# The recurrence of a decoder layer: the y gate kept in two places, its product on VectorE, and the first projection of the merge in two pieces

## What is computed

```python
xc = conv_b + sum(xpad[:, k:k + s] * conv_w[k] for k in range(4))      # causal, per channel
r  = sigmoid(einsum(xc by blocks of 128, w_rg) + b_rg)
ig = sigmoid(einsum(xc by blocks of 128, w_ig) + b_ig)
a  = exp(-8 * r * softplus(-lambda))
gated_x = sqrt(1 - a*a) * (ig * xc)
h  = linear scan over positions:  h[t] = a[t] * h[t-1] + gated_x[t]
o_lru = (h * gelu(yb)) @ w_o_lru
merged = sigmoid(gate_mla) * o_mla + sigmoid(gate_lru) * o_lru
```

## Time and profile before

| | |
|---|---|
| median of 3 runs | 2469.99 us (2469.56 to 2472.95) |
| the profiled execution | span 2469.3 us; the page gives no other time for it |
| PE busy | 2341.7 us, 95% |
| DVE / ACT / POOL busy | 40% / 35% / 14% |
| recurrence, from the first to the last sigmoid of a group | 814.16 to 1003.29 us |

### The profile page before, as it was taken

The page is one execution under the profiler, slowest core; times in us unless marked ns, Lnnn a source line. Parts: engine busy times, 40 slices in busy tenths (PEclk is TensorE's granted clock), DMA queues, the critical chain, the costliest instruction groups (busy, mean ns, idle before and its releaser), DMA issues.

```text
span 2469.3 us, 25993 instructions
## 1 busy us (share of the span) xinstructions
PE 2341.7 (95%) x10629; PEld 1940.8 (79%) x10629; DVE 983.4 (40%) x1089; ACT 859.0 (35%) x1233; POOL 339.0 (14%) x372
## 2 busy tenths in 40 slices
PE   7999999999997999899999788989999999999997
PEld 6888888888786877688887677767888888888885
DVE  3334433432335554211213788465342233322333
ACT  3322223322223666411323566344332223222222
POOL 0000000200003232200012455332210000200002
PEclk9999999999999999999999899999999999999998
DMA  5333433443232111122410100445433423343221
GB/s 179 93 104 100 139 94 94 128 128 102 87 98 77 47 39 48 52 77 68 122 40 20 27 14 21 171 162 167 123 103 102 137 94 94 121 130 107 94 100 62
DMA packets 278016, 232.55 MB, mean 94 GB/s; under 512 B 22853, under 2 KB 250250, under 8 KB 277898
## 3 DMA queue, kind: packets, MB, share of 16 engines
q1 hardware_dynamic: 277898, 230.89, 30.3%
HBM read 209.36 MB, written 20.97 MB: 93 GB/s over the span
## 4 chain that ended last, share of the span: by engine, by line
PE 80%; issue 7%; POOL 5%; DVE 4%; ACT 3%; DMA 1%; SPq 0%; POOLq 0%; ACTq 0%; DVEq 0%
PE ps L85 26%; PE ps L86 26%; PE ps L87 26%; POOL r_xc L841 1%; PE ps L320 1%; POOL r_xc L835 1%; POOL r_xc L838 1%; PE ps L1459 1%; PE ps L1491 1%; ACT a_probs L1435 1%; POOL a_rot L1376 1%; POOL b_sum L1631 1%; ACT w_hi L91 0%; POOL x L287 0%; DVE a_s L1425 0%
## 5 line engine op out<-in xcount | busy, mean ns | idle before, releaser
L85 PE MATMUL ps<-u_hi,w_hi 128*128 128x512 f32 x1920 | 753.0, 392 | 15.5 <-ACT r_gate_y L761 9.5
L87 PE MATMUL ps<-u_hi,w_lo 128*128 128x512 f32 x1920 | 750.9, 391 | 0.0
L86 PE MATMUL ps<-u_lo,w_hi 128*128 128x512 f32 x1920 | 750.8, 391 | 0.0
L95 DVE TENSOR_TENSOR w_lo<-w_raw,w_hi 128x1024 fp32r<-128x1024 f32 (+2 forms) x345 | 426.4, 1239 | 687.9 <-ACT w_hi L91 687.7
L91 ACT ACTIVATE w_hi<-w_raw 128x1024 fp32r<-128x1024 f32 (+2 forms) x345 | 355.3, 1033 | 492.2 <-PE ps L87 452.8
L85 PEld LDWEIGHTS ps<-u_hi,w_hi 128*128 128x128 f32 x1920 | 363.1, 189 | 93.4 <-issue 15.6
L87 PEld LDWEIGHTS ps<-u_hi,w_lo 128*128 128x128 f32 x1920 | 362.5, 189 | 76.1
L86 PEld LDWEIGHTS ps<-u_lo,w_hi 128*128 128x128 f32 x1920 | 362.7, 189 | 74.5
L85 PE MATMUL ps<-w_hi,hs 128*128 128x512 f32 x704 | 275.3, 391 | 12.9 <-DVE hs L95 9.6
L86 PE MATMUL ps<-w_lo,hs 128*128 128x512 f32 x704 | 274.6, 390 | 0.0
L87 PE MATMUL ps<-w_hi,hs 128*128 128x512 f32 x704 | 274.5, 390 | 0.0
(11 more groups left out here) (213 smaller groups left out, 2449.8 us busy)
## 6 DMA issues: line engine op xcount, KB each, us to landing
w_raw<-in_ffn_w_gate_dram SPq DMA_DIRECT2D x88, 512.0 KB, 3.8
w_raw<-in_ffn_w_up_dram SPq DMA_DIRECT2D x88, 512.0 KB, 3.7
w_raw<-in_ffn_w_down_dram SPq DMA_DIRECT2D x88, 512.0 KB, 3.4
w_raw<-in_w_in_dram SPq DMA_DIRECT2D x32, 512.0 KB, 3.8
w_raw<-in_w_out_dram SPq DMA_DIRECT2D x24, 512.0 KB, 3.5
x<-in_x_dram SPq DMA_DIRECT2D x16, 512.0 KB, 6.3
h_scratch<-x SPq DMA_DIRECT2D x16, 512.0 KB, 5.0
x<-h_scratch SPq DMA_DIRECT2D x16, 512.0 KB, 5.2
```

Of the source, the lines that this page charges most:

```text
L85: pe.matmul(out, lh, rh, start=start, stop=False)
L86: pe.matmul(out, lh, rl, start=False, stop=False)
L87: return pe.matmul(out, ll, rh, start=False, stop=stop)
L95: return nc.vector.tensor_tensor(lo, src, as_f32(hi), ALU.subtract)
```

## The change

The gate `gelu(yb)` gets two places, used in turn; the second lies where the low copy of the eighth group will be written. ACT makes `gelu(d+1)` ahead of `out_hi(d)`, and waits only for the product of group d-1. The product with the gate goes from POOL to DVE, behind `w_lo` of y(d+2) and ahead of `out_lo(d)`. PE's `branch_of(0)` is made in two pieces: blocks 0 to 6 of both halves after `out_split` = 7, then block 7 of both halves after `out_split` = 8. As it may now start before the last group is finished, it also waits for the last sigmoid that reads its banks.

```diff
-        self.gate_y = c.at(AT_AREA + 20480, "r_gate_y", [P, SEQ])
+        self.gate_y = [c.at(AT_AREA + at, f"r_gate_y{i}", [P, SEQ]) for i, at in enumerate((20480, 68608 + 4096 * (DK - 1)))]
...
     def gelu(self, act, d):
         self.w.wait_done(act, self.n_y[d])
-        if d > 0:
-            act.wait_ge(self.S["out_done"], d)
-        self.nc.scalar.activation(self.gate_y[:, :], self.c.two(2), ACT.Gelu_apprx_tanh).then_inc(self.S["gelu_done"], 1)
+        if d >= 2:
+            act.wait_ge(self.S["out_done"], d - 1)
+        self.nc.scalar.activation(self.gate_y[d % 2][:, :], self.c.two(2), ACT.Gelu_apprx_tanh).then_inc(self.S["gelu_done"], 1)
...
+    def gated(self, dve, d):
+        to = self.xc[:, d % 2, :]
+        dve.wait_ge(self.S["scan_done"], d + 1)
+        dve.wait_ge(self.S["gelu_done"], d + 1)
+        self.nc.vector.tensor_tensor(to, to, self.gate_y[d % 2][:, :], ALU.mult).then_inc(self.S["out_done"], 1)
...
     def products(self, pool, d):
...
-        pool.wait_ge(self.S["scan_done"], d + 1)
-        pool.wait_ge(self.S["gelu_done"], d + 1)
-        self.nc.gpsimd.tensor_tensor(to, to, self.gate_y[:, :], ALU.mult).then_inc(self.S["out_done"], 1)
...
-    def branch_of(self, pe, d):
+    def branch_of(self, pe, d, chunks=tuple(range(DK))):
         c = self.c
-        self.w.ready(pe, self.n_b[d])
+        if chunks[0] == 0:
+            self.w.ready(pe, self.n_b[d])
         if d >= 2:
             pe.wait_ge(self.S["prod_done"], d - 1)
         else:
-            pe.wait_ge(self.rec.S["out_split"], DK)
+            pe.wait_ge(self.rec.S["sig_i" if d % 2 else "sig_r"], DK)
+            pe.wait_ge(self.rec.S["out_split"], chunks[-1] + 1)
         for hf in range(2):
-            for k in range(DK):
+            for k in chunks:
...
@@ scalar
-                    rec.out_hi(act, d)
                     if d + 1 < DK:
                         rec.gelu(act, d + 1)
+                    rec.out_hi(act, d)
@@ vector
                     if d + 2 <= DK:
                         w.lo(dve, (rec.n_y + [ring[1]])[d + 2])
+                    rec.gated(dve, d)
                     if d == 0:
                         c.norm.all_stored(dve, NT)
                     rec.out_lo(dve, d)
@@ tensor
-                for d in range(DK):
+                lru.branch_of(pe, 0, tuple(range(DK - 1)))
+                lru.branch_of(pe, 0, (DK - 1,))
+                lru.gate_of(pe, 2)
+                for d in range(1, DK):
                     lru.branch_of(pe, d)
```

More of the change, by code:

```diff
@@ L951, in branch_of @@
         else:
-            pe.wait_ge(self.rec.S["out_split"], DK)
+            pe.wait_ge(self.rec.S["sig_i" if d % 2 else "sig_r"], DK)
+            pe.wait_ge(self.rec.S["out_split"], chunks[-1] + 1)
         for hf in range(2):
-            for k in range(DK):
+            for k in chunks:
                 last = mm3(pe, c.ps[:, self.branch_bank(d) + hf, :], self.w.both(self.n_b[d], slice(k * P, (k + 1) * P)),
                            tuple(x[:, k, half_of(hf)] for x in (self.rec.lru_hi, self.rec.lru_lo)), k == 0, k == DK - 1)
-        last.then_inc(self.w.used, 1)
+        if chunks[-1] == DK - 1:
+            last.then_inc(self.w.used, 1)
 class Latents:
```

## The result

The changed kernel takes 2440.24 us at the median of its 4 runs (2436.58 to 2442.65), the kernel before 2470.57 (2469.56 to 2472.95): ratio 0.9875, 95% interval 0.9863 to 0.9887, a gain of 30 us. Run twice more, it gave ratios of 0.9882 (0.9868 to 0.9895) and 0.9872 (0.9855 to 0.9888); its twelve executions together lie between 2435.87 and 2446.07, median 2440.7, and 27 of the kernel before between 2469.02 and 2474.03, median 2471.15. The forecast was 2442.3 with a range of 2440.0 to 2449.6. The median of the first four is just inside it. In the recurrence the mechanism came as foreseen.

What follows compares the result with a forecast made beforehand. PE, 95% busy, was held to 27.23 us a step by the other engines' chain, where it needs 24.48. Standing of 20.4 and lower clock of 7.3 make 27.7 us; 2469.99 - 27.7 = 2442.3 us, range 2440 to 2449.6.

Steps and rivals of the forecast that it cites:

- From 1034.76 on the kernel does the same in the same order: Behind the recurrence, from the start of `gate_of(2)`: nothing changes in the later part, so its term is 0.
- PE's loss of 27.7 us in rows 3, all of it won: From `y_of(2)` to `gate_of(2)`: PE loses 20.4 us standing and 7.3 at lower clock, and the change recovers all 27.7.
- The order of the gelu takes 2.33 us off the chain: ACT in each recurrence step: `w_hi` follows `lru_hi` by 0.96 instead of 3.29 us, and the six gelu waits go.
- The product, 1.22 us on DVE: Gate product moved to DVE: 1.22 us taken, between 0.6 and 3.29; `lru_hi` starts 1.1 us earlier per step.
- PE becomes the bound, with slack that adds up: Recurrence steps: chain 24.0 us against PE's 24.48; once the lead is there the chain needs some 21.6, 2.9 less.
- The cut bridges the tail: `branch_of(0)`: in one piece it would stand about 4 us and lose some 1.5 to lower clock; cutting saves that.
- The seven waits and the 7.3 us of lower clock come back together: Recurrence: removing PE's seven waits, 20.4 us of standing, also returns the 7.3 us of matmuls at 1.2 GHz.
- rival B: Lower clock stays, 2449.6 us, or a later wait takes back a part of that size; chance 0.07.
- rival C: Unbroken 169 us stretch of PE is granted the lower clock, slower than before, up to 2593 us; chance 0.01.
- A: Chain keeps the pace: product on DVE at its upper end, step 26.1 us, gain 17, 2453.0 us; chance 0.08.
- D: `y_of` still waits, as another wait (bank, weights) ends when the gelu does; about 2458 us; chance 0.02.
- The span is 0.7 below the median: Whole kernel: profiled span 2469.3 us set against a run median of 2469.99, from which the gain was subtracted.

## Where the prediction was right, and the step that failed

**The step that failed** is "From 1034.76 on the kernel does the same in the same order": the term for the part behind the recurrence was put at 0 and kept there. It measured -6.5 us in the profiled execution and, by the medians, some -2.7 (2471.15 - 27.7 - 2440.7). The work there is the same; what differs, between 250 and 707 us behind `gate_of(2)`, is PE's running time (396.57 instead of 403.86 us) and the granted clock (0.97 instead of 0.94). The sum for the recurrence held. The later part has a clock of its own, which the forecast took as fixed though the earlier trace rows had just shown what waits do to it. Whether the -2.7 belong to the change or to the spread of that part stays open.

- **PE's loss of 27.7 us in rows 3, all of it won.** Right: 168.64 instead of 196.32.
- **The order of the gelu takes 2.33 us off the chain.** Right. It is worth 15.4 of the 27.7 us when added to the cut ahead of the product, and 8.25 when added last. With it undone steps are 26.1 us and PE waits for the gelu five times.
- **The product, 1.22 us on DVE.** Right, 1.22. Its worth is 2.1 us when added last, 9.3 when added to the cut ahead of the gelu.
- **PE becomes the bound, with slack that adds up.** Right: a sigmoid waits 3.29 us for PE, where 2.9 were worked out, and the chain needs 21.2 us from the seventh sigmoid to the eighth (981.92 - 960.72), forecast 21.6. Doubling the product cost 1.10 us. The last `lru_lo` at 999.57, forecast 1000.2 on a time line that lay 0.32 later.
- **The cut bridges the tail.** Right in place and in the wait (3.7, forecast about 4), too small in the clock behind (2.6, forecast 1.5).
- **The seven waits and the 7.3 us of lower clock come back together.** Right: clock 1.00 from end to end of the stretch. For the recurrence rival B's lower clock, granted whatever PE does, and rival C are out; so are A (steps of 24.48 us) and D (no wait of `y_of`).
- **No other wait in the recurrence.** Right. One thing there I had not named, and it hid: the low copy of the gate weights on DVE takes 1.41 instead of 0.42 us, beside POOL's first product. Nobody waits for it.
- **The span is 0.7 below the median.** A second small error: an execution takes 1.8 us more than its span in every result since (2434.8 and 2436.58). The profiled span of 2469.3 belongs to 2471.1, the median of 27 executions, and not to the 2469.99 of three. By that the forecast would have been 2443.4, further from the 2440.2 and 2440.7 that were measured: this error and the one behind the recurrence partly cancel, so 2442.3 came nearer than its reasoning deserved, by luck. The range's lower end, 2.3 us below the forecast, allowed for the spread of the kernel before (3.4 us in three executions) and not for that of the later part.

## What to carry to other kernels

Where a chain of several engines sets the pace of PE, look for the instruction that PE waits for and ask what stands ahead of it without need: here it was one place of buffer and the order of two lines that together put a gelu, whose input had long been ready, behind a product that it has nothing to do with. Work out both cycles, the chain's and PE's; once PE is the bound, all further shortening of the chain only buys slack, and is worth something at the end alone, where the last group has no work beside it. A comparison of a few us needs a stretch cut at the same instructions in both traces: the totals of the two profiled executions also held 6.5 us from a part whose instructions are the same. And what one piece of a change is worth depends on which pieces are already there (2.1 or 9.3 us for the product).

## What the runs showed of the hardware

- Waits of 1.35 us once in 26 us left TensorE's clock at 1.00. In the recurrence of the kernel before each of the three waits of 1.94 to 2.48 us was followed by matmuls at the lower level. With the cut alone a wait of 1.95 us was not, and three of 2.47 to 2.48 us were. One of 3.7 us cost 2.6 us more in the next 48.
- The same wait can go either way. PE's wait of 2.37 us ahead of the recurrence was followed by clock 0.53 with the gelu behind the copy, and by 1.00 in the changed kernel (3.4 us from the end of the wait):

```profile
793.06:796.50 3.44, 3.44 (x9) 2.72 (x10) 0.00 (x0) 0.00 (x0) 0.00 (x0) 0.53 0.00 0
```

```profile
794.45:797.90 3.45, 3.45 (x15) 2.86 (x16) 0.00 (x0) 0.00 (x0) 0.00 (x0) 1.00 0.00 0
```

- In the attention part the time at the lower level differs between executions of the same program, and the time with it: 0.37 us per us over twelve traces (correlation 0.91).
- Of a DVE operation with two inputs in SBUF and a POOL product that overlap, the second ended as late as if it had begun when the first was done. POOL's 2.34 us became 3.29 behind a `w_lo` that ran to 968.12 (967.09 + 3.29 = 970.38), and DVE's 0.42 became 1.41 us behind a product that ran to 939.86 (938.73 + 1.41 = 940.14).
